# Row dots inside the routes, ten up tiles beside a route, six late tiles

## The reference

```python
q = (hf @ w_q).reshape(t, 8, 2, 64)
s = einsum('thjd,jnd->thjn', q, sub_keys)          # 128 keys a half
sv, si = top_k(s, 16)
comb = sv[:, :, 0, :, None] + sv[:, :, 1, None, :]  # 256 pairs a head
best, pick = top_k(comb, 16)
experts = si[0] * 128 + si[1] of the picked pairs   # 16384 experts
gates = softmax(best)
act = gelu(einsum('td,thkd->thk', hb, u_tab[eb]))
out = einsum('thk,thkd->td', gb * act, v_tab[eb])
```

## Time and profile before

| | us |
|---|---|
| median of three runs | 2411.92 |
| the three runs | 2397.98 to 2414.87 |
| the profiled execution | 2400.55 |
| its span | 2398.6 |
| TensorE busy (with modelled ends) | 2323.9 |
| VectorE busy | 1808.4 |
| ScalarE busy | 1075.6 |
| GpSimd busy | 904.3 |

### The profile page before, as it was taken

How to read it: one execution, slowest core, us unless ns; L and a number is a source line. 1 busy time by engine, 2 the same in 40 slices (tenths; PEclk the granted TensorE clock), 3 DMA queues, 4 the chain that set the end, 5 groups by cost and what they waited for, 6 DMA issues and landing times.

```text
span 2398.6 us, 44667 instructions
## 1 busy us (share of the span) xinstructions
PE 2323.9 (97%) x15004; PEld 2163.4 (90%) x15004; DVE 1808.4 (75%) x3458; ACT 1075.6 (45%) x2062; POOL 904.3 (38%) x515
## 2 busy tenths in 40 slices
PE   7999889999999999999999999999999999999997
PEld 7999669998889999999999998999899999999996
DVE  8985864546958326889998887888578888888887
ACT  6554874466642123433335877787222222222223
POOL 3333455543124433444555443444323223222221
PEclk9999999999999999999999999999999999999998
DMA  3322355433134232334446988899999999999994
GB/s 129 116 79 71 125 189 165 153 114 111 58 106 140 85 122 84 109 121 152 143 157 214 344 321 312 323 330 355 330 339 329 305 306 319 310 307 309 312 309 149
DMA packets 272490, 500.85 MB, mean 209 GB/s; under 512 B 138160, under 2 KB 177104, under 8 KB 271312
## 3 DMA queue, kind: packets, MB, share of 16 engines
q1 hardware_dynamic: 71472, 228.49, 28.4%
q10 hardware_dynamic: 164032, 136.61, 17.5%
q0 software_dynamic: 36864, 134.23, 16.2%
HBM read 423.49 MB, written 76.95 MB: 209 GB/s over the span
## 4 chain that ended last, share of the span: by engine, by line
PE 59%; issue 19%; ACT 8%; DMA 5%; POOL 5%; DVE 2%; ACTq 1%; SPq 0%; POOLq 0%; DVEq 0%
PE ps L1361 25%; PE ps L777 16%; PE ps L1240 11%; POOL wlo L659 4%; PE ps L958 4%; DMA activations<-tmp 3%; ACT rinv L1921 2%; ACT whi L1454 2%; DMA raw<-wt 1%; ACT onehot_i L1925 1%; ACT g_block L1940 1%; PE ps L1326 1%; ACT tmp L1863 1%; PE ps L941 1%; ACTq L1865 1%
## 5 line engine op out<-in xcount | busy, mean ns | idle before, releaser
L1454 ACT ACTIVATE whi<-raw 128x1024 fp32r<-128x1024 f32 x373 | 394.0, 1057 | 953.9 <-PE ps L1361 464.0
L659 POOL TENSOR_TENSOR wlo<-raw,whi 128x1024 fp32r<-128x1024 f32 x179 | 451.6, 2524 | 702.6 <-ACT whi L1454 702.6
L1240 PE MATMUL ps<-h_hi,whi 128*128 128x448 f32 x1008 | 375.2, 372 | 11.2 <-DVE wlo L2720 6.4
L1240 PE MATMUL ps<-h_hi,wlo 128*128 128x448 f32 x1008 | 369.3, 366 | 0.0
L1240 PE MATMUL ps<-h_lo,whi 128*128 128x448 f32 x1008 | 369.3, 366 | 0.0
L1361 PE MATMUL ps<-act_hi,whi 128*128 128x448 f32 x1000 | 365.2, 365 | 0.0
L1361 PE MATMUL ps<-act_lo,whi 128*128 128x448 f32 x1000 | 365.2, 365 | 0.0
L1361 PE MATMUL ps<-act_hi,wlo 128*128 128x448 f32 x1000 | 365.2, 365 | 0.0
L2720 DVE TENSOR_TENSOR wlo<-raw,whi 128x1024 fp32r<-128x1024 f32 x194 | 237.8, 1226 | 152.1 <-ACT whi L1454 141.3
L670 POOL DMA_INDIRECT row<-pv,row_idx x128 | 169.3, 1322 | 459.2 <-DVE row_acc L2750 440.3
L670 POOL DMA_INDIRECT row<-pu,row_idx x128 | 187.1, 1461 | 246.5 <-DVE row L2711 228.1
(11 more groups left out here) (382 smaller groups left out, 4704.6 us busy)
## 6 DMA issues: line engine op xcount, KB each, us to landing
raw<-wt SPq DMA_DIRECT2D x245, 512.0 KB, 3.6
raw<-pv SPq DMA_DIRECT2D x128, 512.0 KB, 6.2
activations<-tmp ACTq DMA_DIRECT2D x128, 224.0 KB
gates_dense<-g_block ACTq DMA_DIRECT2D x7, 4096.0 KB, 14.8
g_tile<-gates_dense ACTq DMA_DIRECT2D x128, 224.0 KB, 4.4
gelu<-activations ACTq DMA_DIRECT2D x128, 224.0 KB, 5.7
a_cum_rows<-decay_sums SPq DMA_DIRECT2D x32, 256.0 KB, 3.3
state_s<-s_in SPq DMA_DIRECT2D x16, 512.0 KB, 6.9
```

Of the source, the lines that this page charges most:

```text
L659: pool.tensor_tensor(lo, raw[n.par][:, :], hi.bitcast(F32), ALU.subtract).then_inc(split_ready, 1)
L1240: mm = pe.matmul(PS[2 * p.par][:, 0:DT], w[slot][:, k, :], x[:, k, 0:DT], start=k == 0 and w is whi and x is HH, stop=k == KD - 1 and w is ...
L1454: act.activation(whi[slot][:, :, :].rearrange("p k c -> p (k c)"), raw[n.par if n.b < N_V else slot][:, :], ACT.Copy)\
```

## The change

The sparse route keeps eight up tiles (ROUTE_0), the four dense routes have ten each (ROUTE_U), and the late stage is left with six instead of 14. Of the 128 up rows 26 are dotted inside the dense routes, 4, 7, 7 and 8 of them (ROWS_R), at points between VectorE's steps; a block of the dense gates has 14 dots (4, 3, 4 and 3 a turn), and four are left for the late stage. The dots wait for `hs_done`, so VectorE waits for it before the first dense route. The four dense routes are written out one after the other on VectorE instead of in a loop. GpSimd waits for the picks before the tenth tile counted from the start of the sparse route and then puts the fetches of 32 rows between the low parts, one after each of the first six and after three of four from then on; the other 96 follow without low parts between them, and then a wait for the last subtraction of the gate stage and the two low parts of the late stage. VectorE's gate loop has three blocks in a body instead of two. ScalarE's exponential comes before the eighth tile of ten, and its loads for the down stage begin after four late tiles.

```diff
-ROUTE_U = 8
+ROUTE_0 = 8
+ROUTE_U = 10
-ROWS_B = 15
+ROWS_R = (4, 7, 7, 8)
+ROWS_B = 14
+ROWS_P = 32
@@ gpsimd
             pool.wait_ge(picks_ready, 1)
-            for k in range(11):
-                low(Idx(N_GU - 9 + k))
-                if k % 2 == 0:
-                    rows(k // 2)
-            for t in range(TURNS):
-                for x in range(4 - t % 4 // 3):
-                    rows(RING + t // 4 * ROWS_B + t % 4 * 4 + x)
+            fetched = 0
+            for k in range(N_GU + 2 - (N_ROUTE + 9)):
+                low(Idx(N_ROUTE + 9 + k))
+                if fetched < ROWS_P and (k < RING or k % 4):
+                    rows(fetched)
+                    fetched += 1
+            for g in range(fetched, ROWS):
+                rows(g)
+            pool.wait_ge(split_ready, N_LU)
             for k in range(2):
                 low(Idx(N_LU + k))
@@ scalar, gate_exp and the late stage
-                for k in range(ROUTE_U):
-                    if k == (ROUTE_U - 2 if isinstance(r, int) else ROUTE_U // 2):
+                for k in range(ROUTE_0 if first else ROUTE_U):
+                    if k == (ROUTE_0 - 2 if first else ROUTE_U - 3):
-            with act.Fori(0, LATE_U // 2 - 3) as i:
-                for k in range(2):
-                    early(Idx(N_LU + k, i, 2), Idx(U_LU + k, i, 2))
+            for k in range(LATE_U - 2):
+                early(Idx(N_LU + k), Idx(U_LU + k))
             for j in range(4):
-                k = LATE_U - 6 + j
-                early(Idx(N_LU + k), Idx(U_LU + k))
                 load_act(j, j)
-            for k in range(2):
-                early(Idx(N_V - 2 + k), Idx(ET - 2 + k))
+                if j % 2:
+                    early(Idx(N_V - 2 + j // 2), Idx(ET - 2 + j // 2))
@@ vector, route
+            def route(c, dots=()):
+                def dot(left):
+                    if len(dots) > left:
+                        s = dots.pop(0)
+                        row_dot(s, s % RING, s // RING)
...
+                    dot(7 - h0 // 2)
...
+                dot(3)
...
+                    dot(2 - s)
+                dot(0)
...
-            route(0).then_inc(parts_ready, 1)
-            with dve.Fori(1, CHUNKS) as c:
-                own.enter(c, 1, 55)
-                route(c).then_inc(parts_ready, 1)
-                own.leave(CHUNKS - 1)
+            dve.wait_ge(hs_done, 1)
+            s = 0
+            for c in range(CHUNKS):
+                route(c, range(s, s + ROWS_R[c])).then_inc(parts_ready, 1)
+                s += ROWS_R[c]
@@ vector, dense gates
+                return ROWS_0 + t // 4 * ROWS_B + (t % 4 * 7 + 1) // 2, 4 - t % 2
...
-            with dve.Fori(0, BLOCKS // 2) as i:
+            with dve.Fori(0, BLOCKS // 3) as i:
```

More of the change, by code:

```diff
@@ L99 @@
 ROWS = P
-ROWS_B = 15
-ROWS_G = ROWS_B * BLOCKS
+ROWS_R = (4, 7, 7, 8)
+ROWS_0 = sum(ROWS_R)
+ROWS_B = 14
+ROWS_G = ROWS_0 + ROWS_B * BLOCKS
+ROWS_P = 32
 P_DT, P_XBC, P_QKV = N_DT, N_XBC, N_GS
@@ L737, in _ @@
                 low(Idx(N_PQ + k))
-            with pool.Fori((N_PQ + 5) // 2, N_GU // 2 - 4) as i:
+            with pool.Fori((N_PQ + 5) // 2, (N_ROUTE + 9) // 2) as i:
                 for k in range(2):
@@ L1297, in turn_parts @@
                 mm.then_inc(parts_turned, 1)
-            for k in range(ROUTE_U):
+            for k in range(ROUTE_0):
                 single(Idx(N_ROUTE + k))
@@ L1900, in gate_exp @@
             def gate_exp(r, L=P):
-                for k in range(ROUTE_U):
-                    if k == (ROUTE_U - 2 if isinstance(r, int) else ROUTE_U // 2):
+                first = isinstance(r, int) and r == 0
+                for k in range(ROUTE_0 if first else ROUTE_U):
+                    if k == (ROUTE_0 - 2 if first else ROUTE_U - 3):
                         act.wait_ge(gmax, r + 1)
                         act.activation(EIJ[0:L, 2, :], EIJ[0:L, 2, :], ACT.Exp).then_inc(gexp, 1)
-                    early(Idx(N_ROUTE + k, r, ROUTE_U), Idx(U_ROUTE + k, r, ROUTE_U))
+                    k0 = 0 if first else ROUTE_0 - ROUTE_U
+                    early(Idx(N_ROUTE + k0 + k, r, ROUTE_U), Idx(U_ROUTE + k0 + k, r, ROUTE_U))
             gate_exp(0)
@@ L2616, in take_turned @@
                     .then_inc(routed, 1)
-            def route(c):
+            def route(c, dots=()):
                 L = P
+                dots = list(dots)
+                def dot(left):
+                    if len(dots) > left:
+                        s = dots.pop(0)
+                        row_dot(s, s % RING, s // RING)
                 for dst, src in ((TVC, TV), (TIC, TI)):
@@ L2679, in sparse_rows, with row_dot @@
                 dve.wait_ge(picks_ready, 1)
-            sparse_rows()
-            route(0).then_inc(parts_ready, 1)
-            with dve.Fori(1, CHUNKS) as c:
-                own.enter(c, 1, 55)
-                route(c).then_inc(parts_ready, 1)
-                own.leave(CHUNKS - 1)
+            def row_dot(s, b, landed):
+                row = GR[b]
+                dve.wait_ge(row_in[b], landed * 16 + 16)
+                dot = DOT[:, s:s + 1] if isinstance(s, int) else DOT[:, bass.ds(s, 1)]
+                dve.scalar_tensor_tensor(row[:, :], row[:, :], 1.0, HS[:, :], ALU.mult, ALU.mult,
+                                         accum_out=dot).then_inc(row_used, 1)
+            sparse_rows()
+            dve.wait_ge(hs_done, 1)
[3 more added lines that the diff above has]
+                s += ROWS_R[c]
             take_turned(CHUNKS - 1)
@@ L2704, in one_hots @@
                     ins.then_inc(hot_ready, 1)
-            def row_dot(s, b, landed):
-                row = GR[b]
-                dve.wait_ge(row_in[b], landed * 16 + 16)
-                dot = DOT[:, s:s + 1] if isinstance(s, int) else DOT[:, bass.ds(s, 1)]
-                dve.scalar_tensor_tensor(row[:, :], row[:, :], 1.0, HS[:, :], ALU.mult, ALU.mult,
-                                         accum_out=dot).then_inc(row_used, 1)
             def low(n):
@@ L2734, in _ @@
                     dve.wait_ge(split_ready, N_GU + 2)
-                hot_turn(t, Idx(N_GU + 2 * t), 4 * t, 4 * t, 4 - t // 3, 0, first=t == 0)
-            with dve.Fori(0, BLOCKS // 2) as i:
-                own.enter(i, 0, 64)
-                for t in range(8):
-                    r = ROWS_B + t // 4 * ROWS_B + t % 4 * 4
-                    n = Idx(N_GU + BLOCK_U + 2 * t, i, 2 * BLOCK_U)
-                    hot_turn(i * 8 + (4 + t), n, i * (2 * ROWS_B) + r, r, 4 - t % 4 // 3, i * (2 * ROWS_B // RING))
-                own.leave(BLOCKS // 2)
+                r, count = rows_of_turn(t)
+                hot_turn(t, Idx(N_GU + 2 * t), r, r, count, 0, first=t == 0)
+            with dve.Fori(0, BLOCKS // 3) as i:
+                own.enter(i, 0, 96)
+                for t in range(12):
+                    r, count = rows_of_turn(t + 4)
+                    n = Idx(N_GU + BLOCK_U + 2 * t, i, 3 * BLOCK_U)
+                    hot_turn(i * 12 + (4 + t), n, i * (3 * ROWS_B) + r, r, count, i * (3 * ROWS_B // RING))
+                own.leave(BLOCKS // 3)
             def row_add(s, b, landed):
```

10 lines of the change are left out of this document (5 added, 5 removed).

## The result

The changed kernel takes 2416.16 us in the median, the kernel before on the same chip 2408.35 (20 runs each). The ratio is 1.0047, 95% interval [1.003, 1.0064], so it is slower by 11 us (7 to 15). I had forecast +2. The time lies inside my range and the change is within 1%, but it is clear of noise and over five times the +2. The profiled execution after took 2415.23 us with a span of 2413.4, against 2400.55 and 2398.6 before: 14.8 us more.

A forecast was written before the change was run, and what follows sets the result against it. TensorE, busy 97% of the span, was taken as the bound. Terms +6 - 1 - 4 + 1 = +2 us gave 2402.5 or 2414 from two base times; the middle, 2408 us, was predicted, range 2392 to 2430.

The forecast's parts named there:

- The cap on a gain: Whole kernel: only idle TensorE time can be won, waits of 13.2 us from 1050 to 1800 us, near 0.6%.
- The tiles: Dense routes: ten up tiles beside each put the transposes about 49.5 us apart, 1186.0 to 1334.5.
- The wait for the token rows: Before route 0: VectorE waits for ScalarE's second copy of the token rows and starts at 1137.0 instead of 1133.1.
- The price of a dot: Dense routes: meeting GpSimd's subtractions adds 0.6 us to a dot's 1.15, 1.75 each, 45.5 us for 26.
- The fetches, costed at nothing: Routes: GpSimd's fetches wait for the dot six before; free while VectorE is on time, otherwise inside the +6.
- The term +6: Dense routes: 26 dots exceed VectorE's 39.9 us of slack by 5.6, taken as +6 us, ends 0 and +52.
- The dense gates, -1: Dense gates: one row less in a block frees queues and VectorE; -1 us, ends 0 and -3.
- The late stage, -4: After the last gate store: three row fetches out of its way, 1 to 1.5 MB; -4 us, ends 0 and -6.4.
- The down start, +1: Start of the down stage: first load needs 9.0 of the 9.8 us ahead; +1 us, ends 0 and +4.4.
- The rival of a late start: Start of the down stage: slowly issued and landing load costs +8.4 instead of +1, total 2417; chance 0.1.
- the anchors: Base times for the sum: profiled execution 2400.55 and median of three runs 2411.92, giving 2402.5 and 2414.
- the three "I am wrong if": Routes cost over 12 us; a VectorE loop end becomes a TensorE wait; gate stage loses or wins over 5 us.

The follow-up runs named there:

- the last kernel: Changed kernel with 22 dots in the routes, fetches at written-out places, loads two tiles earlier, last store halved, ScalarE's gate blocks written out; 2394.75 us, ratio 0.9937.
- the 22-dot kernel: Changed kernel with 22 instead of 26 dots in the routes and fetches from the seventh on at two places of three; 2417.96 us, ratio 1.0069.
- the slots kernel: Changed kernel with 22 dots in the routes and each fetch at a written-out place after which its dot is done; 2403.51 us, ratio 0.9996.
- the one with slots and earlier loads: Changed kernel with 22 dots, fetches at written-out places, and the down stage's loads issued two tiles earlier; 2411.17 us, ratio 1.0008.
- the one with the tiles only: Changed kernel keeping ten tiles a dense route, but with the 26 route dots moved to the late stage; 2437.94 us, one run.

## Why the prediction was wrong, point by point

- **What bounds the kernel: right in the main.** What moved was idle TensorE time and the clock behind it. The cap on a gain was too low: the 13.2 us of waits leave out what the clock costs after them. T to H went from 378.7 to 368.5 when 6.1 of its 7.6 us of waits went, and the last kernel reaches D 14.8 us earlier with 5.8 us of waits left.
- **The tiles: right.** 49.7 us a gap without dots, forecast 49.5, in one execution.
- **The wait for the token rows: right.** Forecast start of route 0 at 1137.0, measured 1137.31.
- **The price of a dot: right in size, 0.65 us for the forecast 0.6** (17.0 us over 26), but largely by luck. It lies elsewhere than I put it. The dots take 1.46 us in the mean but 1.21 in the median, so most are not held; 26 x (1.46 - 1.22) = 6.2 us is theirs. Of the other 10.8, some 9.5 sit in one operation, the division at the end of each route: 10.7 us for four now, 4 x 0.29 before. It stood clear of the subtractions before, and beside them now, and it stands right in front of the transposes. Of the route's other operations some got longer and some shorter, by up to 4.4 us in all four routes.

```profile
L2702 DVE SCALAR_TENSOR_TENSOR row<-row,h_rows x26: 1204/1214/3969, 1159.2 to 1337.2; 128x1024 f32<-128x1024 f32 x26
```

- **The fetches, costed at nothing beside a VectorE in time: wrong.** "Each is ready when its fetch is due, the closest within 1 us" was worked from one route's times. They waited 20.1 us in ten places, and the 22-dot kernel shows 11.8 us lost to it with VectorE in time. The term +6 came out at +7.7 with both causes in it, and they don't add: with either one nearly gone the other cost more (11.8 and 13.9 us between T1 and T4, against 7.9). The size was near, partly by luck; one of its two causes was missed.
- **The dense gates, -1: right in sum (-0.3), for a reason that I didn't give.** I weighed a loop end on VectorE, and none shows up as a TensorE wait. The loop that mattered is ScalarE's, whose code the change only shifted (that the shift is the cause was not tested): one more long wait with no releaser, +3.3 us of missing one-hots, against 2.9 gained on the other two waits.
- **The late stage, -4: the step that failed in kind.** It rested on bytes: 1 to 1.5 MB of fetches off the queues give the tile 3 to 4 us. The tile came 0.5 us sooner and the stretch took 0.6 longer. The store ahead of the tile sets its landing; halving it gave 7.1 us. The three fetches stood 7.3 to 9.8 us behind the store, where six of them cost 0.2 us in another kernel. The earlier trace rows hinted at it: seven stores with different neighbours all landed after 14.2 to 16.3 us.
- **The down start, +1: mis-sized, 6.8.** The rival of a late start had nearly the price (8.4) and the wrong place. Its total of 2417 is also a slip: +9 belongs on the anchors, whose middle then gives 2415, and not on the 2408 that already held +2. I followed the first load to its data, 9.0 of 9.8 us, and it was in time. I did not follow ScalarE's list behind it: seven more issues, one of 2.5 and one of 3.4 us, in front of the next rounding and `tmp`. The earlier trace rows showed the longest issue, 2477 ns, and I used it only in the rival and only once.
- **The sum.** +2 forecast, +14.8 in the profile, 11 by the ratio: late stage 4.6, down start 5.8, routes 1.7 and gates 0.7 make the 12.8 between. A chance of 0.88 for "within 1%" was borne out; but a change worked out as -1, -4, +1 with three unmeasured causes deserved more weight on +5 to +15. My two anchors, 2400.55 and 2411.92, were one run of each of the two groups of the last section, and their middle, 2408, is a time that few runs have.
- **The signs.** The gap after the last store should have been under 3 us and was 4.22. None of the three "I am wrong if" came true: none watched TensorE behind its first down product, where the most was lost against the forecast.

## What to carry to other kernels

When work is moved in front of a transfer's start, follow the whole list of the engine that issues it, not only the first transfer: its later issues stand in front of its own arithmetic. Before giving a transfer time back for bytes taken off the queues, look at what was issued ahead of it; splitting a long store and putting the tile between the halves was worth 7.1 us here, and removing the fetches behind the store half a microsecond. And a loop that an engine runs only twice can cost TensorE 10 us at its jump; a long wait with no releaser at the same instruction of each kernel is the sign.

## What the runs showed of the hardware

**Two paces of the down stage at full granted clock.** The same matmuls, with TensorE busy all the time and a granted clock of 1.00, ran 989 in 200 us in some executions and 969 in others, as in the slots kernel and in the one with slots and earlier loads:

```profile
1800.00:2000.00 200.00, 200.00 (x989) 185.33 (x988) 169.66 (x213) 43.71 (x42) 59.60 (x43) 1.00 0.97 319
```

```profile
1800.00:2000.00 200.00, 200.00 (x969) 181.66 (x969) 165.30 (x206) 43.09 (x41) 50.15 (x42) 1.00 0.94 310
```

Over the stage that is 2% of some 590 us, about 12 us, more than any edit here gave. No kernel was profiled at both paces, but it fits the two groups into which the runs of several kernels fall: the last kernel's nine runs lie at 2383.6 to 2386.7 and at 2394.8 to 2397.8. Before the change 9 of 20 runs are in the lower group (median 2398.0) and 11 in the upper (2411.9); after it 12 (2413.5) and 8 (2424.9). So within the groups the change costs 15.6 and 13.0 us, close to the 14.8 of the profiles. What selects the pace stays open; four of the profiles above have the slower one, and no experiment addressed it.

**A wait of TensorE can cost 1.5 to 1.8 times its length.** 5.4 and 1.2 us of waits in the gates cost 9.9, 4.2 after the store 7.1, and 3.7 at the down start 6.8, each with a granted clock of 0.83 to 0.88 in the window around it. The nine waits in the routes, 6.0 us in all and none over 1.8, cost 7.9, and the granted clock stayed at 1.00.

**Issuing a 224 KB load takes ScalarE 0.53 to 0.56 us in the median and 3.4 us here**, with four value-row fetches (1757.60 to 1762.26) and two weight tiles (1756.21 and 1761.33) issued shortly before. It is no accident of one execution: the longest issue at this place is 3.4 to 3.8 us in five other kernels with this order of the loads, 9.2 in the one with the tiles only, 2.4 in the one with slots, and at most 1.7 in those with the loads two tiles earlier. The medians come from the down stage, where the queues are 95% busy, so busy queues alone are not the cause; which it is wasn't tested.
